# Experts and attention projections in one block, input projections with the context first, merging inputs loaded during the scan

## The chip, the cores and the metric

The kernel runs on one core of one Trainium2 chip. The metric is the device time of one execution in microseconds (us). An execution of the kernel before took 5041.74 us, the median of three (5036.00 to 5061.92). The profile was taken of one more execution, which took 5037.56 us. The engines are called PE (TensorE, matmuls), PEld (its weight loads), DVE (VectorE), ACT (ScalarE), POOL (GpSimd) and SP (SyncE, which here only issues DMAs).

## What is computed

The reference is a two-part denoising network in float32, on 512 latent tokens and 256 context tokens of width 1024. The first block mixes the tokens (a delta-rule recurrence called rwkv and a state-space scan called ssm, both in two directions), merges the two results, and then applies a mixture of 16 experts in which every expert takes the 64 tokens that suit it best. The second block is a windowed attention with a convolutional feed-forward network, then a gated recurrence with another one.

```
hl = rms_norm(x, norm1_pre[l]) * (1 + sc1) + sh1
hc = rms_norm(ctx, norm1_pre[l]) * (1 + csc1) + csh1
mc, ml = mixer(hc, hl, p, rows, ctx_out)
x = x + g1 * rms_norm(ml, norm1_post[l])
h2 = rms_norm(x, norm2_pre[l]) * (1 + sc2) + sh2
x = x + g2 * rms_norm(ec_moe(h2, router[l], exp_w1[l], exp_w3[l], exp_w2[l]), norm2_post[l])
...
hx = rms_norm_2(x, norm1_g[layer]) * (1.0 + sc1) + sh1
hc = rms_norm_2(ctx, norm1_g[layer]) * (1.0 + csc1) + csh1
```

The last two lines are the input of the attention projection `h @ w_in`, with 1536 output columns. It reads the latents `x`, which need the experts' output, and the second block's own context `ctx_2`, which is an input of the whole network and needs nothing computed before it.

## The kernel before

The program is a chain of stages. Each stage is a block: every engine runs a list of its own, in order, and semaphores connect them; between two blocks all engines meet. The stages are small ones for the modulation (`sc`, `ada`), `i` (norm and input projections, `norm_chain`), `rw` (rwkv), `ss` (ssm), `mc` (`merge_chain`), `ex` (`moe`), `q` (`norm_chain` again: residual, norm and attention projections), `at` (attention), `f0`, `hg`, `f1`. Data crosses from stage to stage through DRAM, with one exception: the result `h2` of `mc` stays in SBUF for `ex`.

Activations lie transposed, as 8 tiles (`KD`) of 128 features by tokens: columns 0 to 511 are the latents ("late" below), 512 to 767 the context ("early"). A dense product is done in units (`WeightUnits`): one unit is 128 output features, 1024x128 weights, 512 KB. Each float32 product is three products of parts: `w_hi*x_hi`, `w_hi*x_lo`, `w_lo*x_hi`. ACT casts the high part of a unit (`hi_part`, line 1996), DVE subtracts it from the raw weights for the low part (`lo_part`, line 2001), and PE takes 8 tiles x 3 products x the spans of columns (`tile_products`, line 2008): one of 512 columns and one of 256. Units have 3 slots.

`norm_chain` loads x tile pair by tile pair (latents and context), squares them on ACT, sums the squares on PE with a matrix of ones in full float32 (`RowNorm.total`, line 2481), takes the root on ACT (lines 2494 and 2496), and then goes tile by tile: DVE scales (2953), ACT applies scale and shift for either span (2903) and casts (2905), DVE subtracts (2919), and PE may take that tile. All 768 columns go together, and the second unit follows the first. In stage `q` the same is preceded by the norm of the experts' output (`q_delta`) and by its addition to x (lines 2941 and 2944). Stage `i` also holds the modulation rows, a side job of DVE that runs along with the 84 units.

`ssm` works in 4 groups of heads, each in 12 steps (6 chunks, two directions). In a step from the fifth on, PE makes rows of sums, ACT exponentiates them (line 1085), POOL multiplies (line 1130), and PE multiplies again, two halves per step, with the rows made two halves ahead. During groups 0 to 2, DVE and ACT also prepare the next group (convolution taps); during the last they do not. SP stores a group's output after its last step and then loads the gate input `z` of the next.

`merge_chain` loads three units of `proj_a`, the rwkv output `ya` (2 MB), a gate (2 MB), the ssm output `yb` (4 MB), six small constants and then the further units, all on SP in this order. PE multiplies 8 units with `ya`, 16 with `yb` and 8 of the output projection. ACT waits for the constants before it goes on to the third unit (`consts_done`, line 2666 gives it). A product result of the first 8 units is multiplied with the gate (2683). The norm of `yb` (line 2468 squares, 2474 adds) runs beside them, and `yb`'s parts are made from unit 5 on.

`moe` ends as follows for the last expert: PE multiplies the down projection, ACT copies it out (1475), PE scatters the pair's result to the tokens, 8 tiles (`bring_back`, line 1394), DVE adds them (1535) and POOL stores them to DRAM.

## Time and profile before

| what | value |
|---|---|
| time, median of 3 | 5041.74 us |
| time of the profiled execution | 5037.56 us |
| its span | 5035.8 us |
| PE busy | 4392.4 us, 87% of the span |
| PEld / DVE / ACT / POOL busy | 68% / 50% / 31% / 9% |
| mean granted clock of PE | 0.938 |
| stage i: first projection product to last | 63 to 667 us |
| ssm: last product; mc: first product | 2062 us; 2076 us |
| ex: last product; q: first, last product | 2847 us; 2890 us, 2999 us |

The span is cut by the stages. Within the dense stages PE is busy nearly all the time, so what a change there is worth is read from the stretches in which PE waits, which lie at the stages' beginnings. The granted clock is that of PE, as a share of full speed: after idle time its matmuls take twice as long for a while.

### The profile page before, as it was taken

The numbers are of one execution on the slowest core, as the hardware profiler recorded it, in microseconds if no ns is written. First come the engines' busy times: TensorE is split into PE (matmuls) and PEld (weight loads), VectorE is DVE, ScalarE is ACT, GpSimd is POOL, SyncE is SP. The second block draws the span as 40 slices with busy tenths as digits, with TensorE's granted clock in tenths as the row PEclk, the third lists the DMA queues.
The fourth block names the chain that finished last, engine by engine and source line by source line (L and its number), as shares of the span: only waits on it lengthen the run. The fifth ranks groups of instructions, "written<-read, shape, count | busy, mean of one in ns | idle before, by whom it ended". The sixth has DMA issues, their size and how long they took to land. (4 is left out here: it accounts for less than half of the span.)

```text
span 5035.8 us, 88300 instructions
## 1 busy us (share of the span) xinstructions
PE 4392.4 (87%) x38490; PEld 3427.9 (68%) x38490; DVE 2534.0 (50%) x3709; ACT 1576.3 (31%) x2558; POOL 457.9 (9%) x440
## 2 busy tenths in 40 slices
PE   7999969999998487795999787789999998887999
PEld 5888848888878365573333374468888887676887
DVE  4555667776676565444111325655443322675553
ACT  3222223333332454432000224333222312663332
POOL 0000021111110154100000003310000000000000
PEclk8999979999999699897999998899999999999999
DMA  6656730000000111434999730021222233212232
GB/s 238 234 188 215 258 120 15 15 21 17 15 6 5 53 36 53 148 96 176 421 421 421 278 105 18 18 103 59 63 65 72 78 113 127 83 40 88 88 101 92
DMA packets 163104, 600.01 MB, mean 119 GB/s; under 512 B 24144, under 2 KB 37328, under 8 KB 137376
## 3 DMA queue, kind: packets, MB, share of 16 engines
q1 hardware_dynamic: 148848, 532.49, 29.6%
q0 software_dynamic: 13872, 61.87, 3.1%
q8 instruction: 305, 5.00, 0.4%
q14 instruction: 79, 0.65, 0.0%
HBM read 524.94 MB, written 69.36 MB: 118 GB/s over the span
## 5 line engine op out<-in xcount | busy, mean ns | idle before, releaser
L2008 PE MATMUL f_acc<-f_a_lo,f_w_hi 128*128 128x512 f32 (+1 forms) x4128 | 1040.7, 352 | 49.3 <-DVE f_a_lo L2370 28.4
L2008 PEld LDWEIGHTS f_acc<-f_a_lo,f_w_hi 128*128 128x128 f32 x4128 | 682.9, 190 | 163.0 <-issue 34.5
L2008 PE MATMUL f_acc<-f_a_lo,f_w_lo 128*128 128x512 f32 (+1 forms) x2328 | 706.1, 352 | 0.0
L2001 DVE TENSOR_TENSOR f_w_lo<-f_w_raw,f_w_hi 128x1024 fp32r<-128x1024 f32 (+1 forms) x176 | 228.4, 1298 | 512.6 <-ACT f_w_hi L1996 512.6
L2008 PEld LDWEIGHTS f_acc<-f_a_lo,f_w_lo 128*128 128x128 f32 x2328 | 391.0, 189 | 60.3
L1996 ACT CAST f_w_hi<-f_w_raw 128x1024 fp32r<-128x1024 f32 (+1 forms) x176 | 194.6, 1106 | 576.1 <-DMA f_w_raw<-in_ffn_w_up 203.4
L2008 PE MATMUL i_acc<-i_x_hi,i_w_hi 128*128 128x512 f32 (+1 forms) x1024 | 307.9, 357 | 13.3 <-DVE i_x_lo L2919 9.8
L390 DVE COPY_PREDICATED rw_work<-rw_mask_x,rw_big 128x512 f32<-128x512 uint8 x288 | 238.3, 879 | 157.7 <-PE rw_big L690 152.5
L2008 PE MATMUL i_acc<-i_x_lo,i_w_hi 128*128 128x512 f32 (+1 forms) x1024 | 310.2, 359 | 0.0
L2008 PE MATMUL i_acc<-i_x_hi,i_w_lo 128*128 128x512 f32 (+1 forms) x1024 | 306.0, 355 | 0.0
L1419 PE MATMUL ex_big<-ex_w,ex_xe 128*64 128x512 f32 x1024 | 235.2, 615 | 31.3 <-DMA ex_w<-in_exp_w 30.6
L690 PE MATMUL rw_big<-rw_work,rw_halves 128*64 128x64 f32 x4608 | 260.5, 222 | 0.8 <-issue 0.7
L2764 DVE CUSTOM_DVE_ANT_0 i_sums<-i_mod_rows,i_mod_vec 128x1024 f32<-128x1024 f32 x192 | 236.8, 1234 | 24.1
L687 PE MATMUL rw_big<-rw_halves,rw_work 128*64 128x64 f32 x3840 | 234.2, 222 | 2.3 <-issue 2.3
L690 PEld LDWEIGHTS rw_big<-rw_work,rw_halves 128*64 128x64 f32 x4608 | 228.7, 138 | 1.7 <-issue 1.6
L2001 DVE TENSOR_TENSOR i_w_lo<-i_w_raw,i_w_hi 128x1024 fp32r<-128x1024 f32 x84 | 103.0, 1226 | 215.3 <-ACT i_w_hi L1996 215.2
L687 PEld LDWEIGHTS rw_big<-rw_halves,rw_work 128*64 128x64 f32 x3840 | 203.6, 138 | 2.8 <-issue 2.7
L1419 PEld LDWEIGHTS ex_big<-ex_w,ex_xe 128*64 128x64 f32 x1024 | 76.5, 141 | 187.8 <-issue 153.0
L1542 DVE TENSOR_TENSOR ex_sg<-ex_sg,ex_big 128x512 f32<-128x512 f32 x16 | 11.0, 688 | 379.9 <-ACT ex_sg L1467 379.9
L670 PE MATMUL rw_big<-rw_work,rw_mg 128*64 128x64 f32 x5376 | 190.6, 222 | 11.1 <-DVE rw_mg L386 7.0
L2008 PEld LDWEIGHTS i_acc<-i_x_hi,i_w_hi 128*128 128x128 f32 x1024 | 167.2, 188 | 47.2 <-issue 8.3
L2008 PEld LDWEIGHTS i_acc<-i_x_hi,i_w_lo 128*128 128x128 f32 x1024 | 169.7, 189 | 30.7
(525 smaller groups left out, 7966.8 us busy)
## 6 DMA issues: line engine op xcount, KB each, us to landing
ex_w<-in_exp_w SPq DMA_DIRECT2D x192, 1024.0 KB, 16.4
i_mod_rows<-in_ada_rows SPq DMA_DIRECT2D x128, 512.0 KB, 4.7
f_w_raw<-in_ffn_w_up SPq DMA_DIRECT2D x88, 512.0 KB, 3.5
i_w_raw<-in_w_in_both SPq DMA_DIRECT2D x44, 512.0 KB, 3.6
f_w_raw<-in_ffn_w_down SPq DMA_DIRECT2D x32, 704.0 KB, 4.0
i_w_raw<-in_w_in_lat SPq DMA_DIRECT2D x40, 512.0 KB, 4.6
pt<-i_stage POOLq DMA_DIRECT2D x22, 768.0 KB, 5.9
f_w_raw<-in_hgrn_w_both SPq DMA_DIRECT2D x24, 512.0 KB, 3.5
```

Source lines behind the costliest of these rows:

```text
L390: return dve.copy_predicated(out, mask, data)
L670: last = pe.matmul(in_halves(T_BANK[n % 2], q, m, lv), mg[:, slot(BA, d, c, h), m[0]:m[1]], work_ap(xs_at + ((d * 6 + c) * 2 + h) * CH + ( ...
L687: pe.matmul(in_halves(X_BANK[n % 2], q, m, lv), work_ap(x_at + m[0], [[1, 64]]), t1_ap(n % 2, t_at + (d << lv), split(lv)), start=True, st ...
L690: last = pe.matmul(in_halves(XT_BANK[n % 2], q, m, lv), t1_ap(n % 2, t_at + m[0], [[1, 64]]), work_ap(x_at + ((1 - d) << lv), split(lv)), ...
L1419: last = pe.matmul(big[64 * half:64 * half + 64, 2 * par + m, :], xe[:, kh * KH + k, e * CAP:(e + 1) * CAP], w13[kh][:, m, half, k], start ...
L1542: dve.tensor_tensor(sg[:], sg[:], big[:, 2 * par, :], ALU.mult)
L1996: act.copy(self.view(self.w_hi, u), self.view(self.w_raw, u)).then_inc(self.hi_done, 1)
L2001: dve.tensor_tensor(self.view(self.w_lo, u), self.view(self.w_raw, u), self.view(self.w_hi, u).bitcast(F32), ALU.subtract).then_inc(self.r ...
L2008: op = pe.matmul(acc[:, a:b], part[:, k], xs[:, k0 + k, a:b], start=(first and k == 0 and part is w_hi and xs is x_hi), stop=(last and k = ...
L2764: last = dve.tensor_tensor_reduce(self.junk[:], self.slot[b % self.SLOTS][:], self.vec[:, v], 1.0, 0.0, ALU.mult, ALU.add, self.res[:, b, ...
```

## The change

Four things are edited.

`i`: `norm_chain` handles the context (early) apart from the latents (late). The context's x is loaded and normed first, its 256 columns of the first units (5 slots in place of 3) are multiplied while ACT and DVE norm the latents, and then the first two units (`JOINT`) take the latents' 512 columns tile by tile. Units beyond the slots are as before. The squares are summed step by step (`RowNorm.step`) between other products.

`ss` and `mc`: a `MergeAhead` object gives fixed places in SBUF. During group 1 SP loads `ya` and the first gate, in front of group 3 the first three units of `proj_a`. In the last group's steps ACT and DVE make the high and low parts of these, and at its end ACT applies the sigmoid to the gate. `merge_chain` starts with products; its SP starts with `yb`.

`ex` and `q` become one block, `experts_and_qkv`. The experts' output stays in SBUF (`delta` is `ht`). The context `ctx_2`, x and eight units of weights are loaded into room that the experts give free after their last up projection. In the tail of the last expert the context is squared, summed and normed, eight units take its 256 columns while the residual and the norm of the latents are computed, and then follow the latents as in `i`, with the further four units on all columns. The residual stream `x2` is stored without the context.

`f0` therefore reads its residual with two DMAs, from `x2` and `ctx_2`.

The diff, cut to its core:

```diff
+                    if g == 1:
+                        sp.dma_start(ahead.a_raw[:], ahead.ya).then_inc(next_a_in, 16)
+                        sp.dma_start(ahead.sg[:], ahead.gates[0:KD, :, 0:LAT].rearrange("a p t -> p a t")).then_inc(next_gates_in, 16)
+                    if g == NG - 1:
+                        sp.wait_ge(S["permuted"], 3 * NG)
+                        sp.wait_ge(S["conv_done"], 3 * NG)
+                        for u in range(3):
+                            ahead.w.load(sp, u, next_w_in[u])
...
+                        if not more and s in (3, 5, 7):
+                            ahead.w.lo_part(dve, (s - 3) // 2, next_w_hi, next_w_lo)
+                        if not more and s in (4, 6, 8, 10):
+                            dve.wait_ge(next_a_hi, (s - 4) // 2 + 1)
+                            for k in (s - 4, s - 3):
+                                dve.tensor_tensor(ahead.a_lo[:, k], ahead.a_raw[:, k], ahead.a_hi[:, k].bitcast(F32), ALU.subtract).then_inc(next_a_lo, 1)
...
+                        if not more and s in (1, 3, 5):
+                            ahead.w.hi_part(act, (s - 1) // 2, next_w_in[(s - 1) // 2], next_w_hi)
+                        if not more and s in (2, 4, 6, 8):
+                            if s == 2:
+                                act.wait_ge(next_a_in, 16)
+                                act.wait_ge(S["tr_copied"], TURNS * NG)
+                                act.wait_ge(S["silu_done"], 3 * NG)
+                            act.copy(ahead.a_hi[:, s - 2:s], ahead.a_raw[:, s - 2:s]).then_inc(next_a_hi, 1)
...
+                    if not more:
+                        act.wait_ge(next_gates_in, 16)
+                        act.activation(ahead.sg[:], ahead.sg[:], ACT.Sigmoid).then_inc(next_gates, 1)
...
+                        sp.wait_ge(S["xe_copied"], 2 * KD)
+                        for dst, src in q_consts:
+                            sp.dma_start(dst, src).then_inc(q_loaded, 16)
+                sp.wait_ge(up_ready, 2 * N_EXP)
+                for c in range(2):
+                    k = slice(4 * c, 4 * c + 4)
+                    sp.dma_start(x_e[:, k], columns(x_early_in)[:, k]).then_inc(early_in[c], 16)
+                w.load(sp, 0)
+                for c in range(4):
+                    k = slice(2 * c, 2 * c + 2)
+                    sp.dma_start(x_l[:, k], columns(x_late_in)[:, k]).then_inc(late_in[c], 16)
+                for u in range(1, OUTS):
+                    w.load(sp, u)
 
...
                                                  start=(kh == 0 and k == 0), stop=(kh == 1 and k == KH - 1))
                         last.then_inc(down_ready, 1)
+                pe.wait_ge(q_loaded, 16 * len(q_consts))
+                pe.wait_ge(ye_done, 2 * N_EXP - 2)
+                for k in range(4):
+                    e_norm.step(pe, k)
                 pe.wait_ge(back_done, KD * (PAIRS - 1))
                 pe.wait_ge(S["sel_done"], PAIRS)
                 pe.wait_ge(ye_done, 2 * N_EXP)
-                bring_back(N_EXP, PAIRS - 1, range(KD))
+                for k in range(4):
+                    bring_back(N_EXP, PAIRS - 1, [k])
+                for k in range(4, KD):
+                    e_norm.step(pe, k)
+                bring_back(N_EXP, PAIRS - 1, [4, 5])
+                for k in range(2):
+                    pe.wait_ge(back_done, KD * (PAIRS - 1) + k + 1)
+                    bring_back(N_EXP, PAIRS - 1, [6 + k])
+                    d_norm.step(pe, k)
+                for k in range(2, KD):
+                    d_norm.step(pe, k)
+
+                def q_tile(j, xs, part, k, signal):
+                    a, b = part
+                    w_hi, w_lo = w.view(w.w_hi, j), w.view(w.w_lo, j)
+                    x_hi, x_lo = xs
+                    for wt, xt in ((w_hi, x_hi), (w_hi, x_lo), (w_lo, x_hi)):
+                        op = pe.matmul(acc[j % 3][:, a:b], wt[:, k], xt[:, k], start=(k == 0 and wt is w_hi and xt is x_hi), stop=(k == KD - 1 and wt is w_lo))
+                    if k == KD - 1 and signal is not None:
+                        op.then_inc(signal, 1)
+
+                def early_unit(j, signal=early_done):
+                    if 3 <= j < SLOTS:
+                        pe.wait_ge(e_out, j - 2)
+                    pe.wait_ge(w.ready, j + 1)
+                    for k in range(KD):
+                        if j == 0:
+                            pe.wait_ge(e_ready, k + 1)
+                        q_tile(j, (xe_hi, xe_lo), early, k, signal)
+
+                pe.wait_ge(back_done, KD * PAIRS)
+                early_unit(0)
+                early_unit(1)
+                l_norm.step(pe, 0)
+                early_unit(2)
+                l_norm.step(pe, 1)
+                early_unit(3)
+                l_norm.step(pe, 2)
+                l_norm.step(pe, 3)
+                early_unit(4)
+                l_norm.step(pe, 4)
+                l_norm.step(pe, 5)
+                early_unit(5)
+                l_norm.step(pe, 6)
+                l_norm.step(pe, 7)
+                early_unit(6)
+                early_unit(7)
+                for k in range(KD):
+                    pe.wait_ge(l_ready, k + 1)
+                    for j in range(JOINT):
+                        q_tile(j, (xl_hi, xl_lo), late, k, w.used)
+                for j in range(JOINT, OUTS):
+                    pe.wait_ge(w.ready, j + 1)
+                    if j >= SLOTS:
+                        pe.wait_ge(e_out, SLOTS)
+                    if j >= 3:
+                        pe.wait_ge(t_out[(j - 3) % 2], (j - 3) // 2 + 1)
+                    for k in range(KD):
+                        if j >= SLOTS:
+                            q_tile(j, (xe_hi, xe_lo), early, k, None)
+                        q_tile(j, (xl_hi, xl_lo), late, k, w.used)
 
...
+                    act.wait_ge(early_in[k // 4], 16)
+                    e_norm.square(act, k, x_e[:, k])
+                square_delta(0)
+                square_delta(1)
+                act.wait_ge(consts_done, 1)
+                e_norm.root(act)
+                square_delta(2)
+                square_delta(3)
+                w.hi_part(act, 0)
+                for k in range(4):
+                    shift_part(k, sq_e, 1, xe_hi, e_scaled, e_shifted)
+                    square_delta(4 + k)
+                w.hi_part(act, 1)
+                shift_part(4, sq_e, 1, xe_hi, e_scaled, e_shifted)
+                d_norm.root(act)
+                for k in range(5, KD):
+                    shift_part(k, sq_e, 1, xe_hi, e_scaled, e_shifted)
+                w.hi_part(act, 2)
+                square_late(0)
+                evict_early(0)
+                square_late(1)
+                w.hi_part(act, 3)
+                square_late(2)
+                square_late(3)
+                evict_early(1)
+                w.hi_part(act, 4)
+                square_late(4)
+                evict_early(2)
+                square_late(5)
+                w.hi_part(act, 5)
+                square_late(6)
+                evict_early(3)
+                square_late(7)
+                w.hi_part(act, 6)
+                evict_early(4)
+                w.hi_part(act, 7)
+                l_norm.root(act)
+                for k in range(KD):
+                    shift_part(k, sq_l, 0, xl_hi, l_scaled, l_shifted)
+                    if k in (0, 1, 3):
+                        evict_early((5, 6, None, 7)[k])
+                for j in range(OUTS):
+                    if j:
+                        w.hi_part(act, j + SLOTS - 1)
+                    if j % 2 == 0:
+                        evict(act, act.copy, j)
 
...
+                def residual(k):
+                    dve.scalar_tensor_tensor(delta[:, k], delta[:, k], fac[:, 0, 0, k:k + 1], rstd_d[:], ALU.mult, ALU.mult)
+                    dve.wait_ge(late_in[k // 2], 16)
+                    dve.drain()
+                    dve.tensor_tensor(x_l[:, k], x_l[:, k], delta[:, k], ALU.add).then_inc(x_done, 1)
+
...
+                add_back(N_EXP, PAIRS - 1, range(5))
+                dve.wait_ge(e_norm.rooted, 1)
+                for k in range(3):
+                    early_scale(k)
+                    add_back(N_EXP, PAIRS - 1, [5 + k])
+                w.lo_part(dve, 0)
+                for k in range(KD):
+                    early_low(k)
+                    if k + 3 < KD:
+                        early_scale(k + 3)
+                    if k == 4:
+                        w.lo_part(dve, 1)
+                dve.wait_ge(d_norm.rooted, 1)
+                residual(0)
+                w.lo_part(dve, 2)
+                residual(1)
+                residual(2)
+                w.lo_part(dve, 3)
+                residual(3)
+                residual(4)
+                w.lo_part(dve, 4)
+                residual(5)
+                residual(6)
+                w.lo_part(dve, 5)
+                residual(7)
+                w.lo_part(dve, 6)
+                w.lo_part(dve, 7)
+                dve.wait_ge(l_norm.rooted, 1)
+                for k in range(KD):
+                    q_scale(k, x_l, sq_l, rstd_l, l_scaled)
+                    if k:
+                        q_low(k - 1, sq_l, xl_hi, xl_lo, l_shifted, l_ready)
+                q_low(KD - 1, sq_l, xl_hi, xl_lo, l_shifted, l_ready)
+                for j in range(OUTS):
+                    if j:
+                        w.lo_part(dve, j + SLOTS - 1)
+                    if j % 2:
...
-                sp.dma_start(sg[:], gates[0:KD, :, 0:LAT].rearrange("a p t -> p a t")).then_inc(ga_in, 16)
-                w.load(sp, 2)
                 for c in range(4):
                     k = slice(4 * c, 4 * c + 4)
                     sp.dma_start(b_raw[:, k], yb[:, k]).then_inc(b_in[c], 16)
@@ -2569,7 +2919,7 @@
                 for c in range(KD):
                     if c >= 3:
...
                 act.wait_ge(loaded, 96)
                 act.wait_ge(consts_done, 1)
...
             @block.tensor
             def _(pe):
+                def early_unit(j):
+                    if j >= 3:
+                        pe.wait_ge(*early_evicted(j - 3))
+                    w.products(pe, j, acc[j % 3], x_hi, x_lo, [early], signal=early_done)
+
                 pe.wait_ge(ones_in_done, 16)
                 if post is not None:
-                    d_norm.total(pe, spans[0:1])
-                norm.total(pe, spans)
+                    for k in range(KD):
+                        d_norm.step(pe, k)
+                for k in range(KD):
+                    e_norm.step(pe, k)
+                pe.wait_ge(w.ready, 1)
+                for k in range(KD):
+                    pe.wait_ge(h_ready, k + 1)
+                    last = w.tile_products(pe, 0, acc[0], x_hi, x_lo, [early], k)
+                    if k == KD - 1:
+                        last.then_inc(early_done, 1)
+                    if post is None:
+                        l_norm.step(pe, k)
+                early_unit(1)
+                if post is not None:
+                    for k in range(3):
+                        l_norm.step(pe, k)
+                    for j in range(2, 6):
+                        early_unit(j)
+                        l_norm.step(pe, j + 1)
+                    l_norm.step(pe, KD - 1)
+                for j in range(6 if post is not None else 2, slots):
+                    early_unit(j)
+                for k in range(KD):
+                    pe.wait_ge(h_ready, KD + k + 1)
+                    for j in range(JOINT):
+                        last = w.tile_products(pe, j, acc[j], x_hi, x_lo, [late], k)
+                        if k == KD - 1:
+                            last.then_inc(w.used, 1)
                 for j, (dst, g, toks) in enumerate(outs):
```

## Rows read from the trace of the kernel before

**Rows 1.** The windows view: PE, PEld, DVE, ACT, POOL busy; granted clock; DMA.

```profile
79.40:100.00 20.60, 20.60 (x118) 17.86 (x117) 13.13 (x16) 8.27 (x10) 0.86 (x1) 1.00 0.58 203
...
2103.00:2109.00 6.00, 6.00 (x20) 4.76 (x21) 5.62 (x8) 3.56 (x6) 1.20 (x2) 0.71 0.19 49
```

**Rows 2.** The timeline of PE, matmuls only, at the four hand-offs. Columns: start us, us, idle before.

```profile
44.90 12.23 PE L2481 MATMUL i_sums<-i_sq,i_ones 128*128 128x512 f32 x32 [8.25 <-ACT i_sq L2468]
...
63.35 0.98 PE L2008 MATMUL i_acc<-i_x_hi,i_w_hi 128*128 128x512 f32 x2 [6.22 <-DVE i_x_lo L2919]
...
2076.33 0.77 PE L2008 MATMUL mc_acc<-mc_ya_hi,mc_w_hi 128*128 128x512 f32 x1 [14.10 <-DVE mc_ya_lo L2659]
...
2102.73 0.80 PE L2008 MATMUL mc_acc<-mc_ya_hi,mc_w_hi 128*128 128x512 f32 x1 [13.65 <-DVE mc_w_lo L2001]
...
2840.01 7.11 PE L1394 MATMUL ex_big<-ex_sel,ex_ye 128*128 128x512 f32 x16 [1.37 <-ACT ex_ye L1475]
...
2889.79 0.98 PE L2008 MATMUL q_acc<-q_x_hi,q_w_hi 128*128 128x512 f32 x2 [6.21 <-DVE q_x_lo L2919]
```

**Rows 3.** The timeline of PE where 768, 512 and 256 columns run alone.

```profile
2917.61 0.52 PE L2008 MATMUL q_acc<-q_x_hi,q_w_hi 128*128 128x512 f32 x2
...
2918.67 0.52 PE L2008 MATMUL q_acc<-q_x_hi,q_w_hi 128*128 128x512 f32 x2
...
3403.40 0.62 PE L2008 MATMUL f_acc<-f_a_lo,f_w_hi 128*128 128x512 f32 x2
...
3404.08 0.62 PE L2008 MATMUL f_acc<-f_a_lo,f_w_hi 128*128 128x512 f32 x2
...
3410.92 0.40 PE L2008 MATMUL f_acc<-f_a_lo,f_w_hi 128*128 128x256 f32 x2
...
3411.28 0.40 PE L2008 MATMUL f_acc<-f_a_lo,f_w_hi 128*128 128x256 f32 x2
```

**Rows 4.** The timeline of ACT in the feed-forward stage f0: scale and shift.

```profile
3402.29 0.60 ACT L2235 ACTIVATE f_gate<-f_gate,f_mod,f_fac 128x256 f32<-128x256 f32 x1 [0.49 <-DVE f_gate L2335]
...
3403.27 0.60 ACT L2235 ACTIVATE f_conved<-f_conved,f_mod,f_fac 128x256 f32<-128x256 f32 x1
...
3424.09 0.81 ACT L2235 ACTIVATE f_gate<-f_gate,f_mod,f_fac 128x512 f32<-128x512 f32 x1
...
3427.14 0.81 ACT L2235 ACTIVATE f_sg<-f_sg,f_mod,f_fac 128x512 f32<-128x512 f32 x1
```

**Rows 5.** The scan's end: a DMA's landing, timelines of ACT and POOL, line 1130, a window.

```profile
ss_z<-pt SPq DMA_DIRECT2D x1, 1024.0 KB, 7.6
...
2006.90 1.28 ACT L1085 ACT_TABLE_LOAD   x1 [14.76 <-PE ss_big L1164]
...
L1130 POOL TENSOR_TENSOR ss_seg<-ss_seg,ss_cbt x64: 1262/1453/2903, 1744.1 to 2055.1; 128x512 f32<-128x512 f32 x64
...
1956.84 4.44 POOL L1130 TENSOR_TENSOR ss_seg<-ss_seg,ss_cbt 128x512 f32<-128x512 f32 x2
...
1929.00:1966.00 37.00, 35.45 (x210) 26.51 (x209) 28.27 (x29) 16.87 (x44) 23.48 (x15) 1.00 0.00 1
```

**Rows 6.** The merging stage: timelines of SP, ACT and DVE, and GB/s in slices from 2069.

```profile
2069.44 0.34 SPq L1991 DMA_DIRECT2D mc_w_raw<-in_proj_a  x1
...
2100.37 1.99 ACT L1996 CAST mc_w_hi<-mc_w_raw 128x1024 fp32r<-128x1024 f32 x2 [10.34 <-DVEq L2666]
...
2099.68 0.26 DVE L2662 TENSOR_TENSOR mc_mod<-mc_mod,mc_bias 128x96 f32<-128x96 f32 x1 [16.39 <-DMA mc_gains<-in_norm_pre]
...
GB/s 0 90 270 395 412 412 387 406 399 389 403 373 383 389 389 404 393 389 391 385 381 389 389 389 385 383 389 331 364 399 295 25 4 0 0 25 205 33 8 25
```

**Rows 7.** The page: the low part of a weight unit.

```profile
L2001 DVE TENSOR_TENSOR i_w_lo<-i_w_raw,i_w_hi 128x1024 fp32r<-128x1024 f32 x84 | 103.0, 1226 | 215.3 <-ACT i_w_hi L1996 215.2
```

**Rows 8.** The timeline of DVE: a residual tile of the q stage.

```profile
2868.27 0.75 DVE L2941 SCALAR_TENSOR_TENSOR q_delta<-q_delta,q_fac,q_rstd 128x512 f32<-128x512 f32 x1 [1.49 <-ACT q_rstd L2496]
2869.10 0.69 DVE L2944 TENSOR_TENSOR q_x<-q_x,q_delta 128x512 f32<-128x512 f32 x1
```

More of the change, by code:

```diff
@@ new lines, in evict_early @@
+                def evict_early(j):
+                    act.wait_ge(early_done, j + 1)
+                    act.copy(stage[:, j, LAT:TOK], acc[j % 3][:, LAT:TOK]).then_inc(e_out, 1)
+                for k in range(4, KD):
+                    act.wait_ge(early_in[k // 4], 16)
+                    e_norm.square(act, k, x_e[:, k])
+                square_delta(0)
[3 more added lines that the diff above has]
+                square_delta(2)
@@ L2474, in add, with step @@
             dve.tensor_tensor(self.sq[0], self.sq[0], self.slot(k), ALU.add).then_inc(self.added, 1)
+    def step(self, pe, k):
+        pe.wait_ge(self.squared, k + 1)
+        pe.matmul(self.sums, self.ones[:], self.slot(k), start=(k == 0), stop=(k == self.count - 1)).then_inc(self.taken if k < self.count - 1 else self.summed, 1)
     def total(self, pe, spans):
@@ L2765, in block, with norm_chain @@
         last.then_inc(self.rows_used, 1)
-def norm_chain(nc, name, tokens, x_in, x_out, mods, kinds, gain, shift, scale, ones_in, tail, post=None, rows=None):
-    spans = [(0, LAT)] + ([(LAT, TOK)] if tokens > LAT else [])
+def norm_chain(nc, name, x_late, x_early, x_out, mods, kinds, gain, shift, scale, ones_in, tail, slots, post=None, rows=None):
+    late, early = (0, LAT), (LAT, TOK)
+    spans = [late, early]
+    JOINT = 2
     units, outs = [], []
@@ L2906, in _ @@
-                w.hi_part(act, 1)
+                        act.wait_ge(late_in[k // 2], 16)
+                    l_norm.square(act, k, x[:, k, 0:LAT])
+                if post is not None:
+                    for k in range(KD):
+                        d_norm.square(act, k, delta[:, k])
+                for k in range(KD):
+                    square_early(k)
+                if post is not None:
+                    act.wait_ge(eps_done, 1)
+                    d_norm.root(act)
+                w.hi_part(act, 0)
@@ L2958, in _ @@
+                low_part(KD - 1, late, KD)
+                if post is not None:
+                    evict_early(dve, dve.tensor_copy, 7)
                 if rows is not None:
```

477 lines of the change are left out of this document (325 added, 152 removed).

## The prediction

> **What bounds the kernel now.** I read the page first, then the timeline of PE, the windows and the waits at the stages' edges. PE is busy 87% of the span, and inside a dense stage it has no gap: from 79.4 us it is busy 20.60 of 20.60 us at a granted clock of 1.00, the 2.4 GHz level [rows 1]. What can be won lies in the hand-offs. There are four idle stretches in front of rows of PE [rows 2]: 24 us from the start of stage i (39.3) to its first product at 63.35, with the sums (44.90 to 57.13) inside them; 14.10 before the first product of mc; 13.65 before its third unit; and 40 us from the last experts' product (2847.1) to the first of q at 2889.79. The reader should see there that each wait ends on DVE, the last link of a chain over DMA, ACT and DVE that starts only when its stage starts. The change starts these chains earlier or puts products under them.
>
> **Prices.** One tile step of a unit takes 1.06 us for 768 columns, 0.68 for 512 and 0.36 for 256 [rows 3], so a unit of 8 steps costs 8.48, 5.44 and 2.88. The split costs nothing: 5.44 + 2.88 = 8.32. ACT's scale, shift and cast go at 0.98 us a tile for 256 columns and 3.05 / 2 = 1.52 for 512 [rows 4]. A square of 512 columns is taken at 0.57 (below the 0.81 of scale and shift at that width), so ACT needs 1.55 for an early tile with a late square beside it.
>
> **Stage i.** Removed: the wait of the context for the latents. The context's half loads come first, so the squares begin about 43.5, and 256 columns cost PE half of the old sums. I put the root at 50 (before: 57.1), the first early product at 53. ACT then needs 7 x 1.55 plus one weight cast, so unit 0's early part ends about 65.5, its last latent sum at 66.9. Four more early units take 11.6: 78.5. The latents of units 0 and 1 take 16 x 0.68 = 10.9: 89.4. ACT has been through the late tiles by 86 (8 x 1.52, two casts and four evictions after the root at 68.4), so it hardly delays them. By 89.4 PE has done two whole units and three context parts at 3.04 (8.48 less 5.44): 26.1 us of the old work. Before, it had by then one unit and 10.0 us more: 18.5. Gain 7.6, taken at **7**. Bounds: 3, if the context's loads and root come 4 us late; 11, if PE never waits after 53. The three sigmoids of the side job now sit ahead of the first eviction on ACT; PE wants it 5.4 us after 89.4, ACT gives it about 92. If that cover is gone, it costs what is missing.
>
> **The scan's last group.** SP issues the three weight loads behind the store and the load of z. The z load of 1 MB takes 7.6 us [rows 5], issued at 1995.9; half a megabyte each at some 390 GB/s [rows 6] puts the units at 2005.2, 2006.8 and 2008.3. ACT's list now has two casts of weights and two of `ya` in front of its first exponential, each 1.0 [rows 6]: the cast of unit 1 can end at 2008.2, the next at 2009.3, so the table load begins there and not at 2006.90 [rows 5]. Behind it wait POOL and PE. Cost **2.5**. The later casts and subtractions lie in steps where ACT and DVE idle. The sigmoid of the gate runs under the last transposes and the store. Bounds: 0 (units land 2 us earlier) and 11.5, thus: POOL's product takes 1.26 at best, but 4.44 for two while DVE did taps [rows 5]. If each of the 11 new DVE operations (3 at 1.23 [rows 7], 8 at 0.69 [rows 8]), 9.2 us, stood in POOL's way and POOL in PE's, the group would be 9 longer. But in that very window of taps PE was busy 35.45 of 37.00 [rows 5], since a half's rows are made two halves ahead. So I take nothing. The Trainium skill (SBUF — State Buffer, Who interferes with whom) says that a DVE instruction with two SBUF inputs contends with a GpSimd one that reads SBUF, and that the loser fully blocks. The slow pair agrees; by the rule alone the term would be 11.5, by the window 2.5.
>
> **Stage mc.** Before: SP starts at 2069.44, and 9.7 MB of loads and six constants behind them keep the DMAs at some 390 GB/s until 2099.7; only then DVE has its constants (idle 16.39 for them) and ACT, which had waited 10.34 for DVE, casts the third unit [rows 6]. PE starts unit 2 at 2102.73 at low clock (20 products in 6.00 us, clock 0.71, where full speed makes 26 [rows 1]), so unit 3 begins at about 2102.73 + 5.44 + 1.5 = 2109.7. After, on the same scale: PE starts units 0 to 2 at 2069.6, with one slow start, and is through at 2069.6 + 16.3 + 1.5 = 2087.4. In front of the constants lie only 4.2 MB of `yb`: with the ramp of the first 2 us [rows 6] they and unit 3 land about 2084.5. Constants, cast, the first gate product and subtraction give unit 3 at 2087.6. So the stall goes and unit 3 comes 22 us earlier. What is late next is DVE: norm and parts of `yb`. That chain hangs on unit 5's end and moves with it; I take off 0.5. Gain **21.5**. Bounds: 13 (units 4 and 5, loaded singly behind `used`, late by 4 each) and 24.
>
> **Experts and q.** Moved: consts, context and weights are loaded under the last expert, when DMAs run dry. Its copy-out on ACT waits behind four squares, the fourth of which needs PE's first sum: bring-back starts at 2841.3, not at 2840.01 [rows 2]. A float32 product of 512 columns costs 7.11 / 8 = 0.89 there [rows 2]. PE does bring-back, the context's sums and the delta's; the context's root is out by 2847.8, DVE's scale starts after its fifth addition, ACT shifts from 2851.5. Eight tiles at 0.98, four delta squares and one cast: early unit 0 ends about 2865. The delta's root comes at 2861, and DVE needs 1.44 a residual tile [rows 8] plus 1.23 a unit's low part. From there PE alternates early units (2.88) and latent sums; the last sum ends about 2886, the eighth early unit about 2892. The latent root gives 2887.5; eight tiles at 1.52 plus three evictions of 0.35 end about 2902, the joint latents of units 0 and 1 at 2903.5. Left are six units at 5.44 and four at 8.48, 66.6: the last product at **2970**, before 2999.3. Gain **29**. The early products are hidden nowhere: they are old work, done in old waits. Bounds: 34, PE without a gap from 2841.3 (6.9 bring-back, 17.5 sums, 23.0 early, 43.5 and 33.9: 2966); 22, ACT's and DVE's mixed lists late by 0.9 at each of eight units.
>
> Stores of 1 MB less and one more DMA in f0 lie beside products: nothing.
>
> **Sum.** -7 + 2.5 - 21.5 - 29 = -55.0. On the profiled execution's 5037.6 this is 4982.6; the median of the runs lies 4.2 above that execution, so I predict **4987 us**.
>
> **Rivals.**
> Lists interlock (0.13): in the merged block ACT, DVE and PE wait for each other in turn through eight units, and q gives some 17. For it: ACT and DVE hold about 60% of that stretch. Against: f0 runs this very pattern. Time 4999.
> Merging still waits (0.10): the constants or units 3 to 5 come late, mc gives 13. Time 4995.
> The port decides (0.05): DVE's new operations block POOL and it blocks PE, by the mechanism above, place the last group, 9 more. Time 4996. The rule of the Trainium skill quoted above would have it so.
> The waits close fully (0.07): PE has hardly a gap in all three, 69 in all. Time 4973.
> Nothing to be measured (0.03): two of three hand-offs fail, under 25 us.
> Slower (0.02): the gaps were rest, and without them the clock granted in dense stretches falls. The price is the 4392 us of busy PE; from a fall of 1.3% on (1.00 to 0.987) the gain is gone, at 2% the time is 5070. Against it: no dense window shows other than 1.00 [rows 1].
> The forecast has 0.60, with 4979 to 4995 as its own range.
>
> **Range.** All lower bounds give 3 - 11.5 + 13 + 22 = 26.5 (5015), all upper ones 69 (4973). All low at once is unlikely; 4974 to 5005 leaves out about 2 in 10. A measurement here tells about 0.5% (25 us) from no change. Faster by more 0.95, within 0.03, slower 0.02.
>
> **What would show it.** i: first early product at 53 and PE dense from about 67. The last group: ACT's table load near 2009 and PE 98% busy after. mc: no idle above 2 us before unit 3, which starts 18 after the first product. q: no block edge after the experts, products of 256 columns from about 2853, the last at 2970. Wrong would be: a wait of PE on a low part at each early unit, ACT's constants as a releaser in mc, POOL as one in the scan, or a dense window below 1.00.

## The result and the profile after

The changed kernel takes 5001.07 us (median of 5 runs, 4999.53 to 5004.90) beside 5050.15 us before (5 runs on the same chips, 5036.00 to 5061.92). The ratio is 0.9916, with a 95% interval of 0.9897 to 0.9934: 0.8% faster (the two medians alone give 0.9903, or 49 us; a second comparison, under "the changed kernel again", gives 39). The range of the forecast holds the time; the likeliest value, 4987, lies 14 us below it, and the forecast's own range (4979 to 4995) does not hold it.

The profiled execution of the changed kernel took 5002.31 us with a span of 5000.5, against the 5035.8 that the prediction was made from: 35.3 us less, where its sum says 55.0. Three profiles of the kernel before and two of the changed one (the second and third of before come from the experiments) show where that went. Each stretch ends at the start of the product named, and a cell is its duration in us; the third row holds all of `rw` and the scan's first three groups.

| stretch, up to | before | before, 2nd | before, 3rd | after | after, 2nd | difference of the means | forecast |
|---|---|---|---|---|---|---|---|
| stage i begins to load | 39.2 | 37.8 | 36.1 | 36.3 | 39.3 | 0.1 | 0 |
| last product of i | 627.7 | 620.4 | 620.6 | 615.3 | 615.7 | -7.4 | -7 |
| turns ahead of the scan's last group | 1325.9 | 1330.7 | 1329.2 | 1327.7 | 1320.7 | -4.4 | 0 |
| last product of the scan | 69.2 | 71.5 | 69.1 | 73.6 | 72.8 | 3.3 | 2.5 |
| last product of mc | 214.2 | 214.2 | 214.2 | 197.3 | 197.7 | -16.7 | -21.5 |
| first expert product | 90.1 | 91.8 | 91.8 | 94.5 | 95.0 | 3.5 | 0 |
| last expert product | 471.8 | 470.0 | 470.1 | 472.8 | 472.7 | 2.1 | 0 |
| last product of q | 161.1 | 159.4 | 161.2 | 133.5 | 133.5 | -27.1 | -29 |
| first product of f0 | 339.3 | 337.2 | 338.5 | 338.4 | 338.4 | 0.0 | 0 |
| last product of f0 | 928.1 | 937.2 | 937.4 | 938.1 | 941.3 | 5.5 | 0 |
| last product of hg | 320.4 | 318.6 | 318.8 | 318.5 | 322.2 | 1.1 | 0 |
| last product of f1 | 442.7 | 446.6 | 448.3 | 448.4 | 446.1 | 1.4 | 0 |

The four forecast terms came to -47.9 of the -55.0; the stretches that were to stay the same add 9.4 between them, so the mean profiles differ by 38.5. The row of f0 shows what one profile is worth: the execution that the forecast was scaled to had its f0 9 us shorter than either other one. The row above it hides a spread that only the profiles of the experiments show: the six of kernels without the merged block need 336.7 to 339.3 us there, and of the eight with it four need 338.3 to 338.8 and four 342.2 to 343.4. In those four, two half-clock stretches of PE at the start of attention last 10.2 and 13.7 us and not 3.4 and 10.2. No run isolates why.

PE at the hand-offs in the changed kernel (its timeline, columns as in [rows 2]):

```profile
51.37 0.36 PE L2360 MATMUL i_acc<-i_x_hi,i_w_hi 128*128 128x256 f32 x1 [3.49 <-DVE i_x_lo L3355]
...
2060.54 0.77 PE L2360 MATMUL mc_acc<-mc_ya_hi,mc_ahead_hi 128*128 128x512 f32 x1 [7.34 <-PEq L30]
...
2820.60 3.67 PE L1494 MATMUL ex_big<-ex_sel,ex_ye 128*128 128x512 f32 x8 [0.57 <-ACT ex_ye L1643]
...
2837.69 0.68 PE L1566 MATMUL ex_big<-ex_q_xe_hi,q_w_hi 128*128 128x256 f32 x1
```

Against [rows 2]: the first product of i stands 15 us after its stage's first load (36.3) and not 24; mc begins 7.34 us after the scan, with the change of stages alone in between; its second stall of 13.65 is gone; q's first product comes 17 us after the first bring-back and not 50.

In mc the chain of [rows 6] is still there, DVE first, then ACT:

```profile
2076.12 0.26 DVE L2998 TENSOR_TENSOR mc_mod<-mc_mod,mc_bias 128x96 f32<-128x96 f32 x1 [15.49 <-DMA mc_gains<-in_norm_pre]
...
2076.94 1.05 ACT L2348 CAST mc_ahead_hi<-mc_ahead_raw 128x1024 fp32r<-128x1024 f32 x1 [22.25 <-DMA mc_ahead_raw<-in_proj_a]
```

DVE idles about as long as before (15.49 beside 16.39 us) and ACT longer (22.25 beside 10.34), and PE does not wait for them here: it has three units ready, and is at work on the third until 2079.7, when the fourth, cast at 2076.94, is ready too. In mc's later units it waits 3.5 us in all, 1.5 for low parts of weights and 2.0 for the low part of `yb`.

### The profile page after: what moved, and what is told of

Read it like the earlier page. It is cut to its first block and busy times, and to the rows that moved or that the text cites. A ratio compares the mean times of both kernels' runs of the same rounds, so it can differ in the third digit from the quotient of the medians.

```text
span 5000.5 us, 88385 instructions
## 1 busy us (share of the span) xinstructions
PE 4405.3 (88%) x38490; PEld 3440.6 (69%) x38490; DVE 2542.9 (51%) x3741; ACT 1579.1 (32%) x2606; POOL 456.8 (9%) x436
## 5 line engine op out<-in xcount | busy, mean ns | idle before, releaser
L1519 PE MATMUL ex_big<-ex_w,ex_xe 128*64 128x512 f32 x1024 | 233.6, 611 | 34.2 <-DMA ex_w<-in_exp_w 33.5
L2360 PEld LDWEIGHTS i_acc<-i_x_lo,i_w_hi 128*128 128x128 f32 x1024 | 169.8, 188 | 29.8 <-issue 1.5
```

The source lines that it names most:

```text
L1519: last = pe.matmul(big[64 * half:64 * half + 64, 2 * par + m, :], xe[:, kh * KH + k, e * CAP:(e + 1) * CAP], w13[kh][:, m, half, k], start ...
L2360: op = pe.matmul(acc[:, a:b], part[:, k], xs[:, k0 + k, a:b], start=(first and k == 0 and part is w_hi and xs is x_hi), stop=(last and k = ...
```

## The experiments

**One part alone, and the changed kernel again.** Three kernels take over one part of the change each:

```
 only_i:      norm_chain("i", x, ctx, ..., slots 5)      ssm, merge_chain, moe, norm_chain("q") of before
 only_merge:  ssm(..., ahead), merge_chain(..., ahead)   the rest of before
 only_q:      experts_and_qkv(...), f0 reads [x2, ctx]   the rest of before
```

> The kernel before with the change of stage i alone (context first, five weight slots, two joint units). Theory A (the three hand-offs gain what their stages show, and what is given back in untouched stages belongs to one execution, not to the change): stage i runs from SP's first DMA to its last product in 615 us instead of 627.6; the time is 12 to 16 us below the kernel before, f0's tile step of 768 columns is whichever of 1.04 and 1.06 us the run falls on. Theory B (the give-back is caused by the shift of the stages, each part alone brings some): stage i gains the same 12.7, but f0 shows 1.06 and loses about 7, group 0 of the scan loses about 5, and the time is within 5 us of before.

Measured: 5040.72 us (12 runs) against 5045.68 (28 runs), ratio 0.9992 (0.9981 to 1.0004); the interval holds 1, so the times alone show no gain. The stage took 615.8 us, as A says; the time fell by 5, as B says. The further profiles of before resolve it: in two of the three the old stage i takes 620.5 us, not 627.7, so that 5 is what there is to win against those. It explains the 5 but does not prove it.

> The kernel before with the early loading for merging alone. Theory A: the last group of the scan loses 2.5 to 4.5 us, unit 3 of mc starts 21 us earlier against the scan's end, mc then loses 4 of it because its products stand 235 and not 227 ns apart (the place of the tiles that are loaded ahead); in all the time is 12 us below before. Theory B (the products' distance in mc was chance of that execution): the distance is 227 ns and the time 16 us or more below. Theory C (the new work of DVE and ACT holds up the scan in more than its last group): groups 0 to 2 of the scan lose 6 us as well and the time is within 7 us of before.

Measured: 5034.34 us, ratio 0.9977 (0.9963 to 0.9992), 11 us. mc took 197.7 against 214.2, and three products of mc 0.702 us, as A says. The last group took 71.5 us, 2.3 more than in the first profile of before, but the second profile of before and that of only_i, with no edit in the scan, have 71.5 and 71.4 too: this run alone shows no loss there. The stretch ahead of the last group was 14 us longer than in the first profile of before and 9 longer than in the second. Groups 1 and 2 of the scan make up 6.7 us of the 14. SP's new loads of `ya` and the gate are issued in group 1, so C could be read into it; but groups 1 and 2 of the second profile of before and of only_i, without these loads, take 6.8 us more as well. The time, 11 us down, is not C's either. What the rest of the 14 us is, no run isolates.

> The kernel before with the merged experts and attention projections alone (f0 reads the latents and the context from two tensors). Theory A: from the last experts' product to the last product of q 27 us less than the 152.3 of before; f0's step of 768 columns is whichever of 1.04 and 1.06 us the run falls on; the time is 27 us below before. Theory B (f0 loses by this part's own edit, the two-part load): f0's step is 1.06 and the stage 10 longer; the time is 17 below.

Measured: 5026.41 us, ratio 0.9964 (0.9951 to 0.9976), 19 us. q is 27.6 us shorter than in the first profile (133.5 against 161.1), and f0's step is 1.04: its two-part load is not what lengthened f0 (935.1 us, between the 928.1 and 937.4 of before). The time fell by 19 and not by A's 27; attention, with 343.4 us up to f0's first product, took back 4 to 6 of that. The medians of the three parts give 5.0 + 11.3 + 19.3 = 35.6.

> The changed kernel once more, unchanged, for a second profile. Theory A: the sums of stages differ from the first profile by some us: group 0 of the scan and the experts' start see other stretches at half clock, f0's step of 768 columns can be 1.04 where it was 1.06; mc's products stand again 235 ns apart, because that is the place of its tiles. Theory B (all of it is fixed by the program): f0 has 1.06 again, the scan's group 0 is again 6 us longer than before and each stage is within 1 us of the first profile.

Measured: 5007.02 us, ratio 0.9926 (0.9907 to 0.9945): 38.7 us below the same runs of before that the three parts were measured against, where the parts add up to 35.6. mc's three products take 0.703 again, while the stretch up to the scan's last group is 7 us shorter than in the first profile. A, except that f0 had 1.06 again.

**Why mc's products are slower.** The same products with the same clock take longer in mc after. The tile view (nanoseconds, least, median and most), before, then after:

```profile
L2008 PE MATMUL mc_acc<-mc_yb_hi,mc_w_hi x128: 389/389/628, 2139.0 to 2232.2; 128*128 128x512 f32 x128
```

```profile
L2360 PE MATMUL mc_acc<-mc_yb_hi,mc_ahead_hi x128: 392/397/628, 2109.4 to 2204.8; 128*128 128x512 f32 x128
```

The start of one to the start of the next grows alike, from 226.7 to 234 ns, over 768 products. What differs is the place of the tiles. By the program's own allocation, the tiles of mc's products before begin at multiples of 128 bytes in their partition (yb_hi at 106,624). In the changed kernel MergeAhead's `TOP = 196576` and a rounding to 32 bytes put the activations' tiles, parts of `ya`, `yb` and the merged result, 32 bytes past a multiple of 64 (yb_hi at 96,544). The weights' tiles still begin at multiples of 128; what changed for them is that high and raw parts now alternate.

> The changed kernel with mc's activation tiles moved by 16 to 32 bytes, so that each begins at a multiple of 64 bytes in its partition, as in every other product stage and as in mc before; in the changed kernel they begin 32 bytes past one. Theory A (that offset makes each product of mc slower): the median distance of three 512-column products in mc falls from 0.703 to 0.680 us, mc from unit 8 on is 4 us shorter, the time 3 to 5 us lower than that of the changed kernel (about 5000). Theory B (it is the interleaved weight slots, or the rhythm in which that stage happens to run): the distance stays 0.703 and nothing changes.

```
-    TOP = 196576
+    TOP = 196544
-    a_hi: offset=first + -(-4 * (6 * LAT + 6 * CV_W) // 32) * 32
+    a_hi: offset=first + -(-4 * (6 * LAT + 6 * CV_W) // 64) * 64
-    sb("ahead_room", [P, 6 * LAT + 6 * CV_W])
+    sb("ahead_room", [P, -(-(6 * LAT + 6 * CV_W) // 16) * 16])
```

Measured: 5002.28 us, ratio 0.9917 (0.9903 to 0.9932); three products 0.700, median duration 394 (in both as well, below): almost nothing, as B says. Taken alone that would have ended the matter. But 64-byte tiles are only half way to where before has them, and the opposite test ran beside it:

> The changed kernel with 32 unused bytes ahead of f1's activation tiles, so that these begin 32 bytes past a multiple of 64; the weights stay where they are and the work is the same. Theory A (the offset of the moving tiles costs PE 7.7 ns a product of 512 columns): f1's distance of six products goes from 1.360 to 1.406 us, f1's 1,800 products of that width take 14 us longer, the time is about 5016. Theory B (the offset is nothing to PE): 1.360 and no difference.

```
         w = WeightUnits(ctx, name, units, 3, SPLIT * P)
+        if name == "f1":
+            sb("pad", [P, 8])
```

Measured: 5024.28 us (one run); six products 1.400 us. The tile view of f1, 4700 to 4850 us, after and with the pad:

```profile
L2360 PE MATMUL f_acc<-f_a_lo,f_w_hi x443: 389/389/389, 4699.7 to 4850.0; 128*128 128x512 f32 x148
```

```profile
L2360 PE MATMUL f_acc<-f_a_lo,f_w_hi x430: 393/395/397, 4699.6 to 4849.7; 128*128 128x512 f32 x144
```

32 unused bytes cost f1 10.0 us in its dense part (6.7 ns a product, not the 7.7 expected). The six products take 1.360 us in the other profiles of f1, and the weights stay where they are; all tiles behind them move by the 32 bytes. So the offset of the activations counts, and the next kernel goes to 128:

> The changed kernel with the later casts of the scan's last group, and with the product tiles of mc and of the merged block placed at multiples of 128 bytes (multiples of 64 left mc at 0.700 us for three products of 512 columns). Theory A (a tile of activations or weights off a 128-byte boundary slows each product): mc's three products take 0.680 us again, those of q's last units 0.680 instead of 0.698; mc is 4 us shorter, the merged block 1 to 2, and the time is about 4994. Theory B (something else of the placement or the rhythm of that run): mc stays at 0.700 and the time at about 5000.

```
-    TOP = 196576
+    TOP = 196480
     (the two roundings of a_hi and ahead_room to 128 bytes)
+        sb("pad", [P, 16])
         xe_at = kept_at(nc)
     (and the later casts of the run late_casts, below)
```

```profile
L2367 PE MATMUL mc_acc<-mc_yb_hi,mc_ahead_hi x128: 387/389/500, 2104.7 to 2197.8; 128*128 128x512 f32 x128
```

Measured: 4985.04 us (4 runs), ratio 0.9870 (0.9852 to 0.9888), faster than both kernels. Theory A in mc: 389 ns, 0.680, and mc takes 192.7 us, 5 less than in the changed kernel. The weights lie as in the changed kernel, so their alternating order is not what cost those 5 us. q takes 132.8 (0.7 less), but three products of its units 2 to 6 come to 0.687, from 0.700, and not to the 0.680 of A: there the weights and the latents' low parts moved together, and something is left that no run isolates. More was won where nothing was expected: the experts' products are as long as before, yet they take 465.7 us and not 472.8. Their stage is bound by its weights' transfers (the DMA engines are busy 0.99 of it in the changed kernel, and PE waits 33.5 us for weights), and the page's GB/s in slices 20 to 22 are 420, 421 and 421 in the changed kernel; here they are 424, 427 and 427:

```profile
GB/s 234 257 199 211 260 105 15 15 23 15 15 7 5 54 36 99 113 87 216 424 427 427 228 77 18 25 106 64 64 64 73 82 114 143 57 38 89 90 101 93
```

The pad had moved the tiles that these transfers fill from 64 bytes past a multiple of 128 onto one, and the experts' activations with them. This alone, in the kernel before:

> The kernel before with 64 unused bytes ahead of the experts' tiles, so that the tiles into which their weights are loaded begin at multiples of 128 bytes and not 64 past one; nothing else is changed. Theory A (transfers into tiles off that boundary are slower, which is why the experts became 6 us shorter with the pad): from the first to the last product with the first expert weights 451 us instead of 456 to 458, PE's waits for these weights 27 us instead of 31 to 34, the time some 6 below before. Theory B (that was the chance of one execution): 456 to 458 and no difference.

Measured: 5038.52 us (10 runs) against 5042.68, ratio 0.9989 (0.9976 to 1.0001); the experts' first weight products last 450.8 us. PE's waits in that stage (the view of waits), second profile of before and with the pad:

```profile
PE ex_big L1419 <- DMA ex_w<-in_exp_w: 33.6, 18, 2.8
```

```profile
PE ex_big L1420 <- DMA ex_w<-in_exp_w: 27.9, 17, 2.9
```

A: 5.6 to 7.4 us less in the stage. The same slices of the page show 425, 427 and 427 GB/s, and 420 or 421 in each of the twelve profiles without the pad. The time's interval just touches 1, so the stage shows the effect and the time does not.

**What the last group loses.**

> The changed kernel with the early casts and subtractions four steps later in the scan's last group, behind the first exponentials. Theory A (what that group loses is the list of ACT ahead of its table load, and the clock that falls in PE's longer wait): ACT's table load is out 2.3 us earlier against the group's start, PE's first wait on POOL is 1.1 us as before and not 2.5, and the group loses 0 to 1 us against before instead of 3.6 to 4.5; the time is 3 us below the changed kernel's. Theory B (DVE's new operations block POOL at the port, wherever they stand): POOL's products are at 1.47 us or more beside them, the group loses as much as now.

```
-  ACT casts of weights at s = 1, 3, 5, of ya at 2, 4, 6, 8
+  ACT casts of weights at s = 5, 7, 9, of ya at 6, 8, 10, 11
-  DVE low parts of weights at s = 3, 5, 7, of ya at 4, 6, 8, 10
+  DVE low parts of weights at s = 6, 8, 10, of ya at 7, 9, 11 and behind the loop
```

The timeline of ACT, POOL and PE, and POOL's group of instructions from there to the scan's end (busy us, mean ns), in the changed kernel:

```profile
1995.73 1.28 ACT L1109 ACT_TABLE_LOAD   x1
...
1998.24 3.47 POOL L1157 TENSOR_TENSOR ss_seg<-ss_seg,ss_cbt 128x512 f32<-128x512 f32 x2 [5.52 <-ACT ss_seg L1109]
...
2000.09 1.42 PE L1244 MATMUL ss_big<-ss_xtok,ss_seg 128*128 128x64 f32 x8 [2.51 <-POOL ss_seg L1157]
...
2001.84 1.91 PE L1191 MATMUL ss_big<-ss_tri,ss_kinds 128*128 128x128 f32 x8
```

```profile
L1157 POOL TENSOR_TENSOR ss_seg<-ss_seg,ss_cbt 128x512 f32<-128x512 f32 x16 | 21.2, 1329 | 28.0 <-ACT ss_seg L1109 28.0
```

and with the later casts:

```profile
2004.25 1.10 PE L1250 MATMUL ss_big<-ss_xtok,ss_seg 128*128 128x64 f32 x8 [1.07 <-POOL ss_seg L1163]
...
2005.47 1.05 PE L1197 MATMUL ss_big<-ss_tri,ss_kinds 128*128 128x128 f32 x8
```

```profile
L1163 POOL TENSOR_TENSOR ss_seg<-ss_seg,ss_cbt 128x512 f32<-128x512 f32 x16 | 20.7, 1297 | 25.9 <-ACT ss_seg L1115 25.9
```

Measured: 5000.35 us, ratio 0.9909 (0.9894 to 0.9924), which is not told apart from the changed kernel's, and the group takes 69.1 us: A. In the changed kernel the table load comes 13.5 + 1995.73 - 2006.90 = 2.3 us late against [rows 5] (13.5 is the shift of the two traces just ahead of the group). PE's wait grows by 1.4 to 2.51, and behind the longer wait eight products take 1.91 us instead of 1.05, at half clock.

What this costs depends on how the scan runs. Its group 2 takes 88.8 to 89.0 us in ten of the fourteen profiles and 91.8 to 91.9 in four, whatever the kernel. In the four, the last group takes 71.4 to 71.5 us with the early casts (only_merge, aligned) and without any (the second of before, only_i). In the ten it takes 69.1 to 69.2 without casts, 72.8 to 73.6 with early ones, and 69.1, 69.2 and 71.8 with later ones (late_casts, aligned_128, both). So the early casts cost 3.6 to 4.5 us or nothing.

> The changed kernel with both edits, the tiles at multiples of 64 bytes and the later casts. If each does what theory A of its own run says, the two add up: 6 to 8 us below the changed kernel, about 4996. If neither does, it is the changed kernel again, 5001 to 5007.

Measured: 4995.82 us, ratio 0.9903 (0.9888 to 0.9918). The last group took 71.8 us this time; POOL and ACT show no wait that late_casts doesn't, but PE's clock stayed at 1.2 GHz for 13.7 us at the group's start instead of 10.2. The time is the 4996 of the first expectation, but not by its sum: the tiles on 64 bytes gave next to nothing in aligned, the group did not win what it won in late_casts, and the interval overlaps the changed kernel's.

**The kernel before again.**

> The kernel before once more, unchanged, for a second profile of it. Theory A (the profile that the prediction was made against was one of the fast executions of its kernel, with f0's step of 768 columns at 1.04 us, which 4 of 10 profiles show, and short stretches at half clock): this execution takes 5040 to 5055 us, f0's step is the likelier 1.06, and from the first product of the scan to its last it is 3 to 7 us longer. Theory B (before always has 1.04 in f0 and that scan, and the change costs it both): the same stage times within 1 us, 5037.

> The program of before, instruction for instruction, from a source whose unused classes differ, for a third profile. Expected as for the second: by theory A 5040 to 5055 us with f0's step at 1.04 or 1.06 by chance, by theory B 5037 and 1.04.

Measured: 5043.32 and 5043.19 us; f0's step is 1.06 in both; from the scan's first product to its last they need 9.6 and 5.8 us more than the first profile. A, though 9.6 is above its 3 to 7. The first profile was a good execution of its kernel, and in f0 most of all. But the rhythm works both ways. The tile view of stage i between 120 and 400 us, where code and clock (1.00) are the same, first and second profile of before:

```profile
L2008 PE MATMUL i_acc<-i_x_lo,i_w_hi x528: 284/344/403, 120.2 to 399.2; 128*128 128x512 f32 x88, 128*128 128x256 f32 x88
```

```profile
L2008 PE MATMUL i_acc<-i_x_lo,i_w_hi x540: 274/336/395, 119.8 to 399.8; 128*128 128x512 f32 x90, 128*128 128x256 f32 x90
```

## Where the prediction was right, and which steps failed

The sum's -55.0 came out as -38.5 between the mean profiles; three of its four terms hold. Two steps failed. The term of mc, 21.5, measured 16.7 us, because it priced a unit's products as before and they became slower with the place of their tiles. And the stretches that were put at nothing, on the scale of a single profile, cost 9.4 us: 5.5 in f0, whose 928.1 us in that profile no other profile of before repeats, 3.5 ahead of the experts' first product, and smaller ones of either sign.

**Stage i: right in its mechanism, and in its size partly by luck.** The forecast said 7 and the means give 7.4. Product 300 of the stage stands 77.8 us after the first load and not 84.9, the 7 of the working. The first early product came 15.1 us after that load (forecast 13.7). ACT needs 1.50 us for an early tile with a late square beside it, where 1.55 was reckoned:

```profile
51.20 0.59 ACT L3265 ACTIVATE i_sq<-i_sq,i_mod,i_fac 128x256 f32<-128x256 f32 x1
...
52.70 0.58 ACT L3265 ACTIVATE i_sq<-i_sq,i_mod,i_fac 128x256 f32<-128x256 f32 x1
```

Further on, five weight slots instead of three removed something that the working had missed: PE's waits for low parts of weights, 3.4 us in the view of waits of before, all in the stage's last units, and 0.3 after. Against the profile that it was scaled to, the stage became 12.4 us shorter and not 7. Against this stands the step of 768 columns, 1.04 or 1.06 us, fixed for a stage and an execution and worth 6 us here. The old stage i had the short one in 4 of 6 profiles, the new one in none of 8. Why is open.

**The scan's last group: the cause right, the cost a mean of two cases.** Forecast 2.5 for the late table load, measured 2.3. PE lost nothing by it where the scan runs in its slower rhythm and 3.6 to 4.5 us in the other; 3.3 by the means of five profiles. The working put the three units of weights 1.6 us apart, where half a megabyte at 390 GB/s takes 1.3; that did no harm, for ACT's four casts follow the first unit without a gap (1991.82 to 1995.73).

**mc: the mechanism right, one price wrong (a failed step).** Unit 3 starts 19.2 us after the first product (18 was forecast), and against the scan's end it comes 21.4 us earlier (before 47.9 behind it, after 26.5): the term of 21.5 was there. Then 4.5 us are paid back over the 29 units left, 0.15 a unit. The step that failed is the unspoken one in "on the same scale": it took a unit to cost what it cost before (5.44 us, 0.68 for three products), though the tiles of its activations had moved; three products took 0.703. With the tiles on 128 bytes mc takes 192.7, which is 214.2 less 21.5. The Trainium skill (SBUF — State Buffer, Operand start alignment) says that an operand must start at a multiple of its element size, and that this "is about legality, not speed"; the runs here show the speed, 389 against 397 ns.

**q: right.** All milestones, taken from the last expert product: first bring-back 3.1 us behind it (forecast 3.3), early unit 0 done at 27 (27), the last latent sum at 49.5 (48), the eighth early unit at 55 (54), the joint latents at 66.5 (65.5), the last product at 133.5 (132). PE waited 4.0 us in all, so the rival of interlocked lists was wrong, and so was that of closed waits. 0.7 us of the rest is the place of the tiles. The bound of 34 should read 33: from 2999.3 to its own 2966.

**The port: wrong as a rival.** With all 11 new DVE operations in the group, POOL's 16 products took 1297 ns each, as in before. Placed early, two of them ran beside POOL's first pair:

```profile
1998.23 2.36 DVE L998 TENSOR_TENSOR mc_ya_lo<-mc_ya_raw,mc_ya_hi 128x512 fp32r<-128x512 f32 x2
```

Two such subtractions took 1.29 us in mc before, and POOL's pair took 3.47 us and not 2.94; one product of `xw` took 0.4 more. By the Trainium skill's rule (SBUF — State Buffer, Who interferes with whom) the two contend where both run, and these rows agree. Placed four steps later they did not meet.

**The stretches that were costed at nothing: wrong (the other failed step).** The scale, "the median of the runs lies 4.2 above that execution", rested on three runs. The five medians of before beside these experiments and the result are 5043 to 5050, so the offset is 5 to 13. That alone would make the forecast 4988 to 4995. Between the scan's groups, at the experts' start and in hg, PE's half-clock stretches fall elsewhere when a stage starts elsewhere. The experts' start is the one that looks lasting: 94.5 to 95.0 us in five of the seven profiles of the changed kernel and its variants, 90.1 to 91.8 in the three of before. In that stretch the mean granted clock is 0.62 and 0.60 in the two profiles of the changed kernel, 0.68, 0.65 and 0.65 in those of before, and 0.65 and 0.68 in the two variants (aligned, aligned_128) that need 91.8 and 90.8 us. No part alone shows it (90.8 to 92.0 us), and no run here isolates why. With the spread ahead of f0 it is the part of the miss that stays open. A slower clock in dense stretches, the rival on the other side, did not come: they show 1.00. (Its 2% of 4392 us would be 5075 and not 5070.)

## What to carry to other kernels

Where a tile is placed by hand or behind an odd-sized neighbour, look at its offset modulo 128 bytes: a move that saves a wait can cost every product after it, and in a stage bound by transfers the landing place counts too. A sum of stage gains should take the untouched stages from more than one profile: one execution's f0 was 9 us off here, more than a whole term. When a mending experiment does nothing, run its reverse before giving the cause up: 64 bytes looked like a refutation, and 32 bytes of padding elsewhere showed the effect. And a profile of one part alone needs a profile of the kernel before in the same rhythm beside it, or a change of rhythm is taken for a cost.

## What the runs showed of the hardware

- Products of 512 columns on fp32r parts start 226.7 ns apart where the activations' tiles begin at multiples of 128 bytes, 233 at an odd multiple of 64 and 233 to 234 at 32 past a multiple of 64; the weights began at multiples of 128 throughout (mc, f1). In q, where the weights and the latents' low parts moved from 64 past a multiple of 128 onto one, it went from 233 to 229 only. The experts' float32 products with weights took as long at either place (611 ns in the mean).
- Transfers of 1 MB into tiles that begin 64 bytes past a multiple of 128 run at 420 to 421 GB/s in the page's slices (twelve profiles), into tiles on one at 424 to 427 (two).
- The same code at the same granted clock has two rhythms for alternating products of 512 and 256 columns, 1.04 and 1.06 us for six; it kept through a stretch and changed from one to another, and f0's up units had the shorter in 4 of 14 profiles.
